# One more buffer for each gathered row: a ring of five places for U and ten for V, paid for by reloading shared rows

## The chip, the cores and the metric

One Trainium2 chip, one core. The metric is the device time of one execution in microseconds (us), lower is better. Each version is run several times, and medians are compared. The profile is one execution, recorded by the hardware profiler.

## The reference

Two transformer-like blocks work on 512 tokens of width 1024. Both end in the same kind of sparse mixer ("peer"), which is where nearly all bytes come from:

```
q = (xn @ w_q)                                    # 8 heads, two half keys each
s = q . sub_keys ; top 16 of each half, then top 16 of the 256 sums
es = expert numbers: 8 heads x 16 = 128 experts of each token, out of 16384
act = gelu(einsum('cd,ced->ce', xc, expert_u[ec]))       # 128 dot products of length 1024
out = einsum('ce,ced->cd', gate * act, expert_v[ec])      # weighted sum of 128 rows
```

Block 1 is `h + mixers(rms_norm(h))`, then `h + peer(rms_norm(h) * ln2_g)`, with an S5 state-space mixer and sliding-window attention (128 tokens back). Block 2 has compressed, selected and window attention and a short convolution; its outputs are scaled by rows that are computed from a condition vector (`gt1`, `sc2`, `sh2`, `gt2`): `x = x + gt1 * (mixed @ w_out)`, `h2 = rmsnorm(x, ln_ffn_g) * (1 + sc2) + sh2`, `x = x + gt2 * peer(h2)`, and the result is `rmsnorm(x, ln_final_g)`.

## The kernel before

**Tiles and slots.** The tokens are cut into tiles of 128, so there are eight tiles of work: n = 0 to 3 in layer 1, n = 4 to 7 in layer 2. Each tile needs 128 experts per token. One *slot* is one expert for all 128 tokens of a tile, 1024 slots in all. For slot s GpSimd (`gpsimd_program`) issues one indirect DMA that gathers 128 rows of 8 KB (the U row and the V row of an expert stand next to each other in HBM), 1.05 MB, into the ring. VectorE (`dot`) multiplies the U row with the tile's normed input and sums; ScalarE (`weigh`, for two slots at a time) applies GELU and the gate and makes a small diagonal matrix; TensorE (`vmm`) multiplies it with the V row and adds up in PSUM.

**The ring.** `ring` has NU + NV rows of 1024 numbers in each partition, with NU = 4 and NV = 2 NU. Slot s has its U row at `u_at(s)` and its V row at `v_at(s)`, one in front of the other or behind it in turn, so that one transfer fills both. The gather of slot s may be issued when dot(s - NU) and vmm(s - NV) are done.

**Order.** All five engines run through programs written out in advance. While the slots of tile n - 1 run, the dense work of tile n (norm, projections, attention, routing, top 16) is done in between: `place(n, part, f)` gives the slot at which each piece stands, from the tables `L1_PARTS` and `L2_PARTS`, and `pace` makes an engine do all slots up to there first. Each engine works strictly in its order, so a piece of dense work that takes long, or waits, holds up the slots behind it.

**Weights.** SyncE (`sync_program`) loads the dense weights as units of 512 KB into six places of `wsl`; unit k waits until unit k - 6 is used. `extra(k)` puts other loads in front of unit k, in the same queue.

**Rows.** Several rows of 1024 numbers are held broadcast over all partitions, 4 KB per partition each: `rowA` (the norm's gains, loaded once per layer and in layer 2 multiplied with 1 + sc2), `finr` (first scratch of the condition vector's work, then sc2 as `rsc2`, then the gains of the last norm), `gt1`, `rowB`, `gt2`. `route` makes the normed input X of the peer mixer from `hres` and `rowA`; `wout2` multiplies with `gt1`; `finish` and `finish2` make a finished tile of the output in `fin`, and scale it with `finr`. `kT1` holds the keys of all four tiles of layer 1; `pers` is a large buffer for what must stay.

Of the kernel before, what the change touches and what calls it, by code (L numbers as in the profile page):

```python
# [9 lines left out]
F32 = mybir.dt.float32  # L10
# [6 lines left out]
NU = 4  # L17
NV = 2 * NU
NWS = 6
NSLOT = 1024  # L20
PAIR = 2
# [78 lines left out]
def build(nc, A, out, act_counts):  # L100
    ctx = ExitStack()
    with ctx:
# [51 lines left out]
        finr = sb("finr", [128, D])  # L154
# [5 lines left out]
        rowA = sb("rowA", [128, D])  # L160
        rowB = sb("rowB", [128, D])
        big = sb("big", [128, 5120])
        pers = sb("pers", [128, 13312])
# [5 lines left out]
        modd = nc.dram_tensor("modd", [12, 512], F32, kind="Internal").ap()  # L169
        modr = modd.rearrange("(a b) c -> a (b c)", b=2)  # L170
# [12 lines left out]
        kT1, o = carve(pers, o, 2, 512)  # L183
# [6 lines left out]
        assert o <= 13312, o  # L190
# [38 lines left out]
        gt1, o = carve(pers, o, 1024)  # L229
# [18 lines left out]
        tmp2, o = carve(big, o, 512)  # L248
        gg = cols2[:, 0:24]
# [7 lines left out]
        rsc2 = finr[:, :]  # L257
        bmod = finr[:, 256:768].rearrange("p (b c) -> p b c", c=128)

        def route_bufs(blk):  # L260
            if blk:
                sS, o = carve(pers, at_route, 16, 128)
                halves, base = [sS[:, 0:8, :], sS[:, 8:16, :]], pers
            else:
                halves = [x[:, :].rearrange("p (a b) -> p a b", b=128) for x in (fin, gt2)]
                base, o = rowB, 0
            r = {"halves": halves}
            r["s2"], p = carve(base, o, 256)
            r["cand"], p = carve(base, p, 16, 16)
            r["oh"], o = carve(base, o, 2, 16, 16)  # L270
# [4 lines left out]
            assert o <= (13312 if blk else D), o  # L275
            return r
# [19 lines left out]
        mrow = [finr[:, 0:128], finr[:, 128:256]]  # L296
# [65 lines left out]
        def vector_program(v):  # L362
# [28 lines left out]
            def finish2(n):  # L391
                V.stage("fin")
                V.wait_ge("fsq", n)
                V(v.tensor_scalar(st[:, 2:3], st[:, 2:3], 1.0 / D, 1e-6, ALU.mult, ALU.add))
                V.wait_own()
                V(v.reciprocal(st[:, 2:3], st[:, 2:3]), ("frc", n))
                V.wait_ge("frs", n)
                V.wait_ge("finr")
                V(v.scalar_tensor_tensor(fin[:, :], fin[:, :], st[:, 2:3], finr[:, :], ALU.mult, ALU.mult),
                  ("fout", n))  # L400

            def slots(x):
                back = V.here
                while V.slot < x and V.slot < END:
# [7 lines left out]
                    if k == VL + 4 and n >= 5:  # L412
                        finish2(n - 1)
# [157 lines left out]
            def qk1(n):  # L571
# [26 lines left out]
                V(ts(kT1[:, :, 128 * i:128 * i + 128], PS[2][:, 0:256].rearrange("p (a b) -> p a b", a=2), kgc,  # L598
# [182 lines left out]
            def route(n):  # L781
# [10 lines left out]
                if n == 0:  # L792
                    V.wait_ge("rowA", 0)
                V(v.scalar_tensor_tensor(X, hres[:, i, :], st[:, 1:2], rowA[:, :], ALU.mult, ALU.mult),
# [252 lines left out]
            def wout2(n):  # L1047
# [19 lines left out]
                for b in range(2):  # L1067
# [5 lines left out]
                    V.wait_ge("modrow", 2)  # L1073
# [49 lines left out]
        def scalar_program(a):  # L1123
# [58 lines left out]
            def slots(x):  # L1182
                back = S.here
                while S.slot < x and S.slot < END:
# [9 lines left out]
                    if k == VL + 4 and n >= 5:  # L1194
                        finish2(n - 1)
# [118 lines left out]
            def route(n):  # L1314
# [5 lines left out]
                rstd(n, "r", 1, hres[:, i, :], xr[:, :])  # L1320
                pace(n, "route", 0.3)
# [134 lines left out]
        def tensor_program(t):  # L1456
# [143 lines left out]
            def scores1(n, g):  # L1600
# [8 lines left out]
                for r in range(4):  # L1609
                    k0 = 128 * (n - 1) + s0  # L1610
                    x = t.matmul(PS[r // 2][:, 256 * (r % 2) + s0:256 * (r % 2) + 256],
                                 xT[64 * a_:64 * a_ + 64, 4 * m + r, :],
                                 kT1[64 * a_:64 * a_ + 64, m, k0:128 * (n + 1)], start=True, stop=True)
# [335 lines left out]
        def sync_program(s):  # L1949
# [20 lines left out]
            def extra(k):  # L1970
# [7 lines left out]
                if (n, name, b, u) == (0, "glu", 0, 0):  # L1978
                    load(rowA[:, :], A["ln2_g"].broadcast_to([128, D]), "rowA", 0)
# [16 lines left out]
                if (n, name, b, u) == (4, "win", 3, 0):  # L1996
                    for q in range(4, 12):
                        Y.wait_ge("modo", q)
                    load(rsc2, modr[4:5, :].broadcast_to([128, 1024]), "modrow", 4)
                    Y.wait_ge("X", 3)  # L2000
                    load(rowA[:, :], A["ln_ffn_g_2"].broadcast_to([128, D]), "lnf")
# [7 lines left out]
                if n >= 4 and (name, b, u) == ("win", 4, 0):  # L2009
                    Y.wait_ge("h", n - 1, 1)  # L2010
                    Q(s.dma_start(cw, A["conv_w_2"][0, :, 0, :].unsqueeze(0).broadcast_to([128, 3, 512])), "cw",
                      ("cw", n))
                if (n, name, b, u) == (4, "wout", 0, 0):
# [4 lines left out]
                    load(gt1, modr[2:3, :].broadcast_to([128, 1024]), "modrow", 2)  # L2018
# [3 lines left out]
                if (n, name, b, u) == (5, "win", 0, 0):  # L2022
                    Y.wait_ge("rowA", 1)
                    load(finr[:, :], A["ln_final_g_2"].unsqueeze(0).broadcast_to([128, D]), "finr")
# [14 lines left out]
            for k in range(NWS, len(units)):  # L2039
                extra(k)  # L2040
                unit(k)

# [127 lines left out]
```

## Time and profile before

| what | before |
|---|---|
| median of 3 runs | 3549.24 us (3537.84 to 3552.84) |
| the profiled execution's own time | 3552.45 us |
| its span | 3551.0 us |
| moved by DMA | 1343.61 MB, 378 GB/s over the span |
| busy share TensorE / VectorE / ScalarE / GpSimd | 70 / 67 / 39 / 30% |

The page cuts the span into 40 slices and gives for each the share of time in which the core's 16 DMA engines were busy, and the GB/s that they moved. Tables by windows give the same for any stretch. Their DMA share is the sum of the packets' times over 16 engines; a few percent of overlap make it read up to 1.02 where no engine is idle. GpSimd is listed as POOL, VectorE as DVE, ScalarE as ACT, TensorE as PE (its weight loads as PEld), SyncE as SP.

### The profile page before, as it was taken

The page shows a single profiled execution, that of the slowest core. Times are in us where ns is not written, and L with a number is a line of the kernel's source. Part 1 is how long each engine was busy: PE and PEld are TensorE (multiplying, and loading weights), DVE is VectorE, ACT ScalarE, POOL GpSimd, SP SyncE. Part 2 cuts the span into 40 slices and gives each one's busy share as a digit, 9 for nine tenths or more (in the row PEclk, how much of TensorE's full clock was granted, in tenths as well). Part 3 has the DMA queues.
Part 4 walks back from the last instruction along what each step waited for, and adds up shares of the span by engine and source line. Part 5 has one row for each costly group of instructions (what it writes and reads, how often), then busy time and mean ns, then how long its engine had stood idle before and what let it go on. Part 6 is the DMA issues. An engine that isn't in the chain of part 4 may idle for free.

```text
span 3551.0 us, 40113 instructions
## 1 busy us (share of the span) xinstructions
PE 2498.8 (70%) x13640; PEld 977.6 (28%) x13640; DVE 2390.7 (67%) x5690; ACT 1370.3 (39%) x3648; POOL 1078.5 (30%) x1038
## 2 busy tenths in 40 slices
PE   7768669676696776866577667767677668765555
PEld 3433233222332223322222223222232223311111
DVE  7438873687835878467664886668775887666664
ACT  1113332344323443233283335534383436533332
POOL 0001332223322233332333323332333323333332
PEclk9689779798797987988778888888888888977777
DMA  7659999999999999999999999999999999999998
GB/s 241 218 200 375 369 355 406 416 408 393 359 396 416 416 391 355 385 394 396 380 409 395 399 398 394 395 400 414 374 401 393 393 394 401 387 386 393 396 407 336
DMA packets 228013, 1343.61 MB, mean 378 GB/s; under 512 B 28360, under 2 KB 33768, under 8 KB 95968
## 3 DMA queue, kind: packets, MB, share of 16 engines
q0 software_dynamic: 148320, 1076.50, 76.0%
q1 hardware_dynamic: 78816, 262.43, 19.3%
q8 instruction: 107, 1.75, 0.2%
q10 hardware_dynamic: 672, 2.12, 0.1%
q14 instruction: 98, 0.80, 0.1%
HBM read 1338.24 MB, written 2.71 MB: 378 GB/s over the span
## 4 chain that ended last, share of the span: by engine, by line
DMA 31%; PE 26%; DVE 17%; issue 15%; POOL 5%; ACT 4%; SPq 0%; POOLq 0%; ACTq 0%; DVEq 0%
DMA ring<-in_k_uv,idx 15%; PE ps L1543 12%; DMA ring<-in_k_vu,idx 12%; PE ps L1472 9%; DVE ring L372 6%; POOL ring L1944 5%; DMA wsl<-in_k_wu 4%; DVE big L420 2%; ACT L1128 1%; PE ps L1525 1%; PE ps L1681 1%; DVE rowB L420 1%; ACT diag L1128 1%; ACT xr L1128 1%; PE ps L1627 1%
## 5 line engine op out<-in xcount | busy, mean ns | idle before, releaser
L372 DVE CUSTOM_DVE_ANT_0 ring<-ring,xn 128x1024 f32<-128x1024 f32 x1024 | 1243.7, 1222 | 654.3 <-DMA ring<-in_k_uv,idx 351.7
L1472 PE MATMUL ps<-ring,diag 64*64 64x512 f32 x8192 | 1272.2, 741 | 518.9 <-ACT diag L1128 474.9
L1944 POOL DMA_INDIRECT ring<-in_k_vu,idx x512 | 530.7, 1036 | 1267.2 <-DVE aw L372 673.7
L1944 POOL DMA_INDIRECT ring<-in_k_uv,idx x512 | 541.7, 1058 | 1109.5 <-DVE aw L372 855.9
L1543 PE MATMUL ps<-wsl,xT 128*128 128x512 f32 (+1 forms) x1536 | 730.1, 622 | 77.9 <-DMA wsl<-in_k_wu 54.1
L1472 PEld LDWEIGHTS ps<-ring,diag 64*64 64x64 f32 x8192 | 304.8, 158 | 1240.8 <-ACT diag L1128 725.2
L1128 ACT ACTIVATE aw<-aw 128x2 f32<-128x2 f32 x512 | 103.9, 203 | 1320.1 <-DVE aw L372 1314.6
L1128 ACT ACT_TABLE_LOAD x375 | 481.1, 1283 | 64.2 <-DVE big L420 51.8
L1543 PEld LDWEIGHTS ps<-wsl,xT 128*128 128x128 f32 x1536 | 291.7, 200 | 528.1 <-issue 437.8
L1128 ACT ACTIVATE diag<-gid,aw 128x64 f32<-128x64 f32 x1024 | 306.3, 341 | 129.6 <-PE ps L1472 112.9
L1128 ACT ACTIVATE gid<-ident,gate 128x64 f32<-128x64 f32 x1024 | 292.5, 332 | 0.0
L1681 PE MATMUL ps<-pers,rowB 128*128 128x64 f32 x224 | 51.3, 421 | 106.1 <-DVE rowB L678 81.6
L1525 PE MATMUL ps<-ident,big 128*128 128x128 f32 x288 | 60.1, 332 | 81.9 <-DVE big L420 31.7
L420 DVE TENSOR_TENSOR big<-ps,big 128x512 f32<-128x512 f32 x40 | 27.6, 690 | 107.6 <-PE ps L1543 107.3
L1525 PE MATMUL ps<-ident,xr 128*128 128x128 f32 x208 | 37.1, 334 | 85.7 <-DVE xr L424 64.4
L372 DVE DVE_READ_ACCUMULATOR2_ANT aw<- 128x1 f32 x1024 | 83.9, 82 | 0.0
L1681 PEld LDWEIGHTS ps<-pers,rowB 128*128 128x128 f32 x224 | 48.7, 329 | 118.4 <-issue 118.4
L1525 PEld LDWEIGHTS ps<-ident,big 128*128 128x128 f32 x288 | 38.0, 164 | 137.3 <-ACT big L1128 60.6
L1128 ACT ACTIVATE xr<-ps 128x512 f32<-128x512 f32 x32 | 18.2, 589 | 144.6 <-PE ps L1543 141.1
L420 DVE TENSOR_TENSOR big<-big 128x512 f32<-128x512 f32 x84 | 58.2, 693 | 20.0 <-ACT big L1128 17.1
L1863 PE MATMUL ps<-pers,big 128*128 128x64 f32 x320 | 48.9, 288 | 23.9 <-DVE big L1024 23.9
L420 DVE TENSOR_TENSOR big<-ps,pers 128x512 f32<-128x512 f32 (+5 forms) x120 | 58.1, 494 | 3.5 <-PE ps L1627 2.8
(227 smaller groups left out, 2033.9 us busy)
## 6 DMA issues: line engine op xcount, KB each, us to landing
wsl<-in_k_wu SPq DMA_DIRECT2D x408, 512.0 KB
wsl<-in_k_wmod SPq DMA_DIRECT2D x48, 512.0 KB
ring<-in_k_vu,idx POOLq DMA_INDIRECT x512
ring<-in_k_uv,idx POOLq DMA_INDIRECT x512
wsl<-in_k_wu SPq DMA_DIRECT2D x16, 280.0 KB
big<-in_b_gate SPq DMA_DIRECT2D x4, 1024.0 KB, 11.7
big<-in_conv_w SPq DMA_DIRECT2D x4, 768.0 KB
hres<-in_x SPq DMA_DIRECT2D x4, 512.0 KB, 7.7
```

Of the source, the lines that this page charges most:

```text
L372: V(v.tensor_tensor_reduce(u_row(s), u_row(s), xn[:, b, :], 1.0, 0.0, ALU.mult, ALU.add, aw[:, b, k:k + 1]), ("dot", s))
L420: return v.tensor_tensor(out, a_, b_, op)
L1128: return a.activation(out, in_, f, **kw)
L1472: r = t.matmul(PA[half][64 * q:64 * q + 64, :], diag[64 * half:64 * half + 64, s % (2 * PAIR), :], v_row(s)[64 * half:64 * half + 64, 512 ...
L1525: r = t.transpose(PS[bank][:, j * 128:(j + 1) * 128], s_, ident[:, :])
L1543: r = t.matmul(PS[bank][:, 0:nn], lhsT(kk_), wsl[:, at % NWS, j, 0:nn], start=(kk_ == 0), stop=(kk_ == nk - 1))
L1627: x = t.matmul(PS[2 + b][:, 256 * h + 128 * z:256 * h + 128 * z + 128], BT[32 * j:32 * j + 32, 4 * z + c, :], uT[32 * j:32 * j + 32, c, :] ...
L1681: x = t.matmul(PS[4 + h // 8][:, 64 * (h % 8):64 * (h % 8) + 64], PT1[:, r, 128 * k:128 * k + 128], v1[:, (n + 1 + k) % 2, 64 * g:64 * g + ...
L1863: r = t.matmul(PS[4 + br][:, 64 * h:64 * h + 64], PT2[:, k % 2, 128 * j:128 * j + 128], vsn[:, j, 128 * br + 64 * g:128 * br + 64 * g + 64 ...
L1944: Q(p.indirect_dma_start(out=both_rows(s), out_offset=None, in_=tab, in_offset=bass.IndirectOffsetOnAxis(ap=idx[:, n % 2, k:k + 1], axis=0 ...
```

## The change

It raises NU from 4 to 5, so the ring has 15 rows for 12 (12 KB more in each partition). The room comes from four places:

- `rowA` is gone. The norm's gains are loaded anew for each tile into `fin` (called `lnr`), just before the unit `wq` 0 0. In layer 2 the product of gains and 1 + sc2 is made once, at tile 4; ScalarE writes it to DRAM (`lnd`), and tiles 5 to 7 load it from there.
- `finr` is gone. The gains of the last norm are loaded for tile 4 and tile 5 into `xr`, and once for tiles 6 and 7 into a place of `wsl` when the weights are used up. For tiles 4 to 6 `finish2` moves from slot 8 to slot 20 of the next tile.
- `gt1` no longer stays in `pers`; it is loaded for each tile of layer 2 into a part of `big` that attention uses, after attention is done (`o1`, n, 1). sc2 goes beside it at tile 4.
- `kT1` keeps two tiles of keys. In an odd tile they stand in order; in an even tile the two halves are swapped, and one score product of 256 columns becomes two of 128.

```diff
-NU = 4
+NU = 5
 NV = 2 * NU
...
-        kT1, o = carve(pers, o, 2, 512)
+        kT1, o = carve(pers, o, 2, 256)
...
+        gt1, _ = carve(big, o2 + 1024, 1024)
+        lnr = fin[:, :]
+        def finr(n):
+            return xr[:, :] if n < 6 else wsl[:, 0, :, :].rearrange("p a b -> p (a b)")
...
-                    if k == VL + 4 and n >= 5:
+                    if k == (20 if n < 8 else VL + 4) and n >= 5:
                         finish2(n - 1)
...
+                V.wait_ge("lnr", n)
                 if n == 4:
-                    V.wait_ge("lnf")
                     V.wait_ge("modrow", 4)
-                    V(v.scalar_tensor_tensor(rowA[:, :], rsc2, 1.0, rowA[:, :], ALU.add, ALU.mult), ("rowA", 1))
+                    V(v.scalar_tensor_tensor(lnr, rsc2, 1.0, lnr, ALU.add, ALU.mult), ("lnf",))
...
+                if n == 4:
+                    S.wait_ge("lnf")
+                    Q(a.dma_start(lnd, lnr[0:1, :]), "lnd", ("lnd",))
...
+                    if n % 2:
+                        x = t.matmul(PS[r // 2][:, 256 * (r % 2):256 * (r % 2) + 256], q,
+                                     kT1[64 * a_:64 * a_ + 64, m, :], start=True, stop=True)
+                    else:
+                        for k in range(s0 // 128, 2):
+                            x = t.matmul(PS[r // 2][:, 256 * (r % 2) + 128 * k:256 * (r % 2) + 128 * k + 128], q,
+                                         kT1[64 * a_:64 * a_ + 64, m, 128 * (1 - k):256 - 128 * k],
+                                         start=True, stop=True)
...
-                    load(gt1, modr[2:3, :].broadcast_to([128, 1024]), "modrow", 2)
...
+                if n >= 4 and (name, b, u) == ("wout", 1, 0):
+                    Y.wait_ge("o1", n, 1)
+                    Q(s.dma_start(gt1, modr[2:3, :].broadcast_to([128, 1024])), "gt1", ("gt1", n))
+                    if n == 4:
+                        load(rsc2, modr[4:5, :].broadcast_to([128, 1024]), "modrow", 4)
+                if (name, b, u) == ("wq", 0, 0):
+                    if n < 4:
+                        Y.wait_ge("s5b", n, 1)
+                        row = A["ln2_g"]
...
+                    else:
+                        Y.wait_ge("lnd")
+                        if n >= 6:
+                            Y.wait_ge("out", n - 2)
+                        row = lnd
+                    Q(s.dma_start(lnr, row.broadcast_to([128, D])), "lnr", ("lnr", n))
+                if n >= 6 and (name, b, u) == ("win", 4, 0):
+                    last_row(n - 2)
```

On SyncE's queue, from the second half of tile 5's input projection to that of tile 6's, before (`wsl` is the weights, `in_conv_w` the convolution's taps; the 33 units are 8 of win, 8 of wout, 8 of wq, 1 of sk, and 8 of the next tile's win):

```order
L2011 DMA big<-in_conv_w 128x1536
L1962 DMA wsl<-in_k_wu 128x1024 x33
L1962 DMA wsl<-in_k_wu 128x2x280 x4
L1962 DMA wsl<-in_k_wu 128x1024 x4
L2011 DMA big<-in_conv_w 128x1536
```

The same stretch of the changed kernel's SyncE queue, where `big<-modd` is gt1, `fin<-lnd` the norm's row and `xr<-in_ln_final_g` the last norm's gains for tile 4:

```order
L2021 DMA big<-in_conv_w 128x1536
L1974 DMA wsl<-in_k_wu 128x1024 x12
L2033 DMA big<-modd 128x1024
L1974 DMA wsl<-in_k_wu 128x1024 x4
L2048 DMA fin<-lnd 128x1024
L1974 DMA wsl<-in_k_wu 128x1024 x17
L1974 DMA wsl<-in_k_wu 128x2x280 x4
L1974 DMA wsl<-in_k_wu 128x1024 x4
L2021 DMA big<-in_conv_w 128x1536
L2055 DMA xr<-in_ln_final_g 128x1024
```

The run of 33 units is now cut in three: the second half of `wout` stands behind gt1 and its wait for the end of attention, and `wq` stands behind the norm's row.

In layer 1, the same queue from tile 0's GLU weights to the end of tile 1's units, before (`in_b_gate` is the gate's bias, `in_k_bmod` the condition vector's, `in_k_wmod` its weights):

```order
L1962 DMA wsl<-in_k_wu 128x1024 x41
L1989 DMA big<-in_b_gate 128x2048
L1962 DMA wsl<-in_k_wu 128x1024 x24
L1954 DMA finr<-in_k_bmod 128x512
L1962 DMA wsl<-in_k_wu 128x1024 x33
L1962 DMA wsl<-in_k_wmod 128x1024 x16
```

And in the changed kernel:

```order
L1974 DMA wsl<-in_k_wu 128x1024 x24
L2048 DMA fin<-in_ln_g 128x1024
L1974 DMA wsl<-in_k_wu 128x1024 x17
L2000 DMA big<-in_b_gate 128x2048
L1974 DMA wsl<-in_k_wu 128x1024 x24
L1966 DMA pers<-in_k_bmod 128x512
L1974 DMA wsl<-in_k_wu 128x1024 x24
L2048 DMA fin<-in_ln_g 128x1024
L1974 DMA wsl<-in_k_wu 128x1024 x9
L1974 DMA wsl<-in_k_wmod 128x1024 x16
```

One load of 512 KB has come in ahead of the nine units `wq` and `sk` of every tile.

## Rows read from the trace of the kernel before

**Rows 1.** The page: engines' busy time; DMA by slices; the gathers' queue.

```profile
PE 2498.8 (70%) x13640; PEld 977.6 (28%) x13640; DVE 2390.7 (67%) x5690; ACT 1370.3 (39%) x3648; POOL 1078.5 (30%) x1038
DMA  7659999999999999999999999999999999999998
GB/s 241 218 200 375 369 355 406 416 408 393 359 396 416 416 391 355 385 394 396 380 409 395 399 398 394 395 400 414 374 401 393 393 394 401 387 386 393 396 407 336
q0 software_dynamic: 148320, 1076.50, 76.0%
```

**Rows 2.** Windows: width, busy us by engine, PEclk, DMA share, GB/s.

```profile
267.00:3531.00 3264.00, 2302.64 (x12774) 875.05 (x12776) 2247.12 (x5324) 1320.62 (x3544) 1068.36 (x1020) 0.83 0.98 393
3233.00:3245.00 12.00, 7.06 (x36) 1.61 (x32) 5.17 (x11) 1.78 (x8) 3.75 (x5) 0.64 1.01 422
```

**Rows 3.** Windows around gaps of the DMA engines, three of 26.

```profile
402.00:408.00 6.00, 6.00 (x36) 1.99 (x29) 4.89 (x10) 2.09 (x8) 2.90 (x3) 0.69 0.53 172
...
1379.00:1386.00 7.00, 7.00 (x44) 3.47 (x44) 6.11 (x12) 2.44 (x10) 2.73 (x3) 0.79 0.52 186
...
3224.00:3229.00 5.00, 3.61 (x16) 0.80 (x16) 3.50 (x8) 3.10 (x8) 2.62 (x2) 0.54 0.63 218
```

**Rows 4.** Timeline, tile 1's attention, around 396 to 409 us.

```profile
396.77 0.94 POOL L1944 DMA_INDIRECT ring<-in_k_uv,idx  x1 [1.54 <-DVE aw L372]
...
397.96 3.65 PE L1681 MATMUL ps<-pers,rowB 128*128 128x64 f32 x16 [7.04 <-issue]
...
400.25 1.23 DVE L372 CUSTOM_DVE_ANT_0 ring<-ring,xn 128x1024 f32<-128x1024 f32 x1
...
401.54 5.73 PE L1472 MATMUL ps<-ring,diag 64*64 64x512 f32 x32
...
402.79 1.23 DVE L372 CUSTOM_DVE_ANT_0 ring<-ring,xn 128x1024 f32<-128x1024 f32 x1
...
404.33 1.24 POOL L1944 DMA_INDIRECT ring<-in_k_uv,idx  x1 [6.62 <-DVE aw L372]
```

**Rows 5.** Timeline, tile 6's convolution, around 2500 to 2512 us.

```profile
2500.63 1.22 DVE L372 CUSTOM_DVE_ANT_0 ring<-ring,xn 128x1024 f32<-128x1024 f32 x1
...
2502.12 1.15 POOL L1944 DMA_INDIRECT ring<-in_k_vu,idx  x1 [3.76 <-DVE aw L372]
...
2506.41 1.22 DVE L372 CUSTOM_DVE_ANT_0 ring<-ring,xn 128x1024 f32<-128x1024 f32 x1
...
2507.90 1.68 POOL L1944 DMA_INDIRECT ring<-in_k_vu,idx  x1 [4.63 <-DVE aw L372]
```

**Rows 6.** Waits of VectorE in tile 2's attention, 801 to 979 us: total, times, longest.

```profile
DVE ring L372 <- DMA ring<-in_k_vu,idx: 11.9, 11, 3.3
DVE ring L372 <- DMA ring<-in_k_uv,idx: 11.5, 15, 3.0
```

**Rows 7.** Timeline of GpSimd before and after the first dot product.

```profile
251.50 0.94 POOL L1944 DMA_INDIRECT ring<-in_k_vu,idx  x1 [0.30 <-issue]
286.67 0.94 POOL L1944 DMA_INDIRECT ring<-in_k_uv,idx  x1 [34.24 <-DVE aw L372]
```

**Rows 8.** Timeline, output projection and routing of tile 6.

```profile
2664.28 0.69 DVE L420 TENSOR_TENSOR big<-big 128x512 f32<-128x512 f32 x1
...
2675.87 15.99 SPq L1962 DMA_DIRECT2D wsl<-in_k_wu  x8
...
2683.16 3.70 PE L1543 MATMUL ps<-wsl,xT 128*128 128x512 f32 x8
...
2695.69 1.28 DVE L794 SCALAR_TENSOR_TENSOR xn<-hres,st,rowA 128x1024 f32<-128x1024 f32 x1 [1.16 <-ACT st L1128]
```

**Rows 9.** Issue to landing of the gate's bias; queues in 2680 to 2698 us.

```profile
big<-in_b_gate SPq DMA_DIRECT2D x4, 1024.0 KB, 11.7
...
q0 software_dynamic: 666, 4.86, 65.3%
q1 hardware_dynamic: 708, 2.60, 35.8%
```

More of the change, by code:

```diff
@@ L20 @@
 NSLOT = 1024
+PERS = 12192
 PAIR = 2
@@ L153, in build @@
         gt2 = sb("gt2", [128, D])
-        finr = sb("finr", [128, D])
         xT = sb("xT", [128, 8, 128])
@@ L159, in build @@
         cols3 = sb("cols3", [128, 2, 8])
-        rowA = sb("rowA", [128, D])
         rowB = sb("rowB", [128, D])
         big = sb("big", [128, 5120])
-        pers = sb("pers", [128, 13312])
+        pers = sb("pers", [128, PERS])
         rflat = ring[:, :, :].rearrange("p a b -> p (a b)")
@@ L189, in build @@
         snk, o = carve(pers, o, 16)
-        assert o <= 13312, o
+        mrow = [carve(pers, o + 128 * k, 128)[0] for k in range(2)]
+        bmod, o = carve(pers, o + 256, 4, 128)
+        assert o <= PERS, o
         gt, o = carve(big, 0, 2048)
@@ L228, in build @@
         zprev, o = carve(pers, o, 512)
-        gt1, o = carve(pers, o, 1024)
         at_route = o
@@ L255, in build @@
         o3 = o1r.rearrange("p (h d) -> p h d", d=64)
-        rsc2 = finr[:, :]
-        bmod = finr[:, 256:768].rearrange("p (b c) -> p b c", c=128)
+        rsc2, _ = carve(big, o2, 1024)
         def route_bufs(blk):
@@ L295, in build @@
         assert o <= 3328
-        mrow = [finr[:, 0:128], finr[:, 128:256]]
         first = [carve(rflat, 512 * k, 4, 128)[0] for k in range(3)]
@@ L397, in finish2 @@
                 V.wait_ge("frs", n)
-                V.wait_ge("finr")
-                V(v.scalar_tensor_tensor(fin[:, :], fin[:, :], st[:, 2:3], finr[:, :], ALU.mult, ALU.mult),
+                V.wait_ge("finr", n)
+                V(v.scalar_tensor_tensor(fin[:, :], fin[:, :], st[:, 2:3], finr(n), ALU.mult, ALU.mult),
                   ("fout", n))
@@ L1072, in wout2 @@
                     V.wait_ge("wout", n, b)
-                    V.wait_ge("modrow", 2)
+                    V.wait_ge("gt1", n)
                     V(tt(x, PS[4 + b], gt1[:, 512 * b:512 * b + 512], ALU.mult), ("wo_e", n, b))
@@ L1193, in slots @@
                         finish(n - 1)
-                    if k == VL + 4 and n >= 5:
+                    if k == (20 if n < 8 else VL + 4) and n >= 5:
                         finish2(n - 1)
@@ L1609, in scores1 @@
                 for r in range(4):
[L1610 to L1613, printed above, removed]
+                    q = xT[64 * a_:64 * a_ + 64, 4 * m + r, :]
+                    if n % 2:
[6 more added lines that the diff above has]
+                                         start=True, stop=True)
                 T(x, ("a_sc", n, g))
@@ L2010, in extra @@
                     Y.wait_ge("h", n - 1, 1)
+                    if n == 5:
+                        Y.wait_ge("lnf")
                     Q(s.dma_start(cw, A["conv_w_2"][0, :, 0, :].unsqueeze(0).broadcast_to([128, 3, 512])), "cw",
@@ L2021, in extra, with last_row @@
                     load(gt2[:, :], modr[5:6, :].broadcast_to([128, 1024]), "modrow", 5)
-                if (n, name, b, u) == (5, "win", 0, 0):
-                    Y.wait_ge("rowA", 1)
-                    load(finr[:, :], A["ln_final_g_2"].unsqueeze(0).broadcast_to([128, D]), "finr")
+                if n >= 4 and (name, b, u) == ("wout", 1, 0):
[7 more added lines that the diff above has]
+                        row = A["ln2_g"]
+                    elif n == 4:
+                        Y.wait_ge("gate", 3, 7)
+                        row = A["ln_ffn_g_2"]
+                    else:
[6 more added lines that the diff above has]
+                    last_row(n - 2)
+            def last_row(*tiles):
+                if tiles[0] < 6:
+                    Y.wait_ge("perm", tiles[0])
+                Q(s.dma_start(finr(tiles[0]), A["ln_final_g_2"].unsqueeze(0).broadcast_to([128, D])), "finr",
+                  *[("finr", n) for n in tiles])
             load(hres[:, 0, :], A["x"][0, 0:128, :], "x", 0)
@@ L2041, in sync_program @@
                 unit(k)
+            for k in range(len(units) - NWS, len(units)):
+                Y.wait_ge("unit_used", k)
+            last_row(6, 7)
         for engines in ((Blank(),) * 5, (nc.vector, nc.scalar, nc.tensor, nc.gpsimd, nc.sync)):
```

13 lines of the change are left out of this document (4 added, 9 removed).

## The prediction, made before the changed kernel ran

> **What bounds the kernel now.** I read the page first, for the busy shares. No compute engine is near full: VectorE is busy 67% of the span [rows 1]. The DMA row is another matter: nearly all slices after the third read 9, and the gathers (q0) alone take 76.0% of the 16 engines' span [rows 1]. So the next view is the windows. Between the first dot product and the last gather, 267 to 3531 us, the DMA share is 0.98 and the rate 393 GB/s; in a stretch without a gap the share reads 1.01 and the rate 422 GB/s [rows 2]. The kernel is bound by its bytes, 1077 MB of them gathered. What is left over is (a) a hundredth or two of the time in which DMA engines have nothing queued and (b) stretches at full share whose packets are slower than the best. A ring of more places can only win back (a).
>
> I then went through the span in narrow windows and looked for gaps. There are 26 of them between 400 and 3230 us: 12 in the attention of tiles 1 to 3 (four per tile, one for each group of heads), the others in layer 2's convolution, compression and output stages and in the last tile's top 16; [rows 3] show the first, the deepest and the last. A window loses its width times (1 - share): 6 x 0.47 = 2.8 us, 7 x 0.48 = 3.4 and 5 x 0.37 = 1.9 us. Summed in the same way the 26 give 58.7 us. The stretch as a whole loses 3264 x 0.02 = 65 us (share rounded to 0.01, so 49 to 82), so the gaps are nearly all there is of (a).
>
> The timeline tells why a gap opens. In tile 1's attention GpSimd issues a gather at 396.77 and the next at 404.33 us [rows 4], 7.6 us later, where one gather takes 1.05 MB / 422 GB/s = 2.5 us. The row names a dot product as releaser, but dots kept coming, at 400.25 and 402.79 for instance; what had been missing is on TensorE, where the attention's products stand at 397.96 and the late `vmm`s of four slots (8 matmuls each) follow in one block at 401.54 [rows 4]. The gather of s waits for vmm(s - 8). In tile 6's convolution it is VectorE: one dot at 2500.63, the next at 2506.41, the convolution's element-wise work in between, and GpSimd's issues lie 5.8 us apart [rows 5]. Both are bursts, no lack of capacity: in the 178 us of tile 2's attention with its four gaps VectorE still waits 11.9 + 11.5 = 23.4 us for gathered rows [rows 6]. It has time to catch up once the rows are there.
>
> **The change part by part.**
>
> *The ring.* With five U rows and ten V rows the gather of s waits for dot(s - 5) and vmm(s - 10). At the start of each burst one more gather is in flight, worth 2.5 us of DMA time, and two more slots of `vmm` may be late. A gap of g us becomes max(0, g - 2.5). Of the 26, twelve are longer than 2.5 us, by 4.0 us together (0.9 for the longest). So 58.7 - 4.0 = 54.7 us are won if each burst finds the ring full; the waits of [rows 6], 6 us for each gap, say that it does. At the other end, if TensorE's block of late `vmm`s only moves, half of that, 27 us. I take 54.7. Once, at the start, four gathers are issued by 251.50 and the fifth waits 34.24 us for the first dot [rows 7]; that one now comes early too: 2.5 us.
>
> *More bytes.* Before there are five broadcast loads of 512 KB among the rows concerned (rowA twice, gt1, sc2, finr). Now there are sixteen: 8 for the norm's row, 4 of gt1, 1 of sc2, 3 of the last norm's. Eleven more, all in the DMA-bound stretch: 11 x 0.524 MB / 393 GB/s = 14.7 us. These are paid in full, since nothing hides a byte where the DMA engines bound the time.
>
> *SyncE's waits.* The unit `wout` 1 0 and all behind it now stand behind o1(n, 1). In tile 6 attention ends at 2664.28 + 0.69 = 2664.97, and TensorE wants the second half of wout from 2683.16 on [rows 8]: 18.2 us. In this time gt1 and two units must land, 3 x 0.524 = 1.57 MB. Where both queues have work, SyncE's moves 2.60 MB in 18 us, 144 GB/s [rows 9], so 10.9 us. To this I add 4.4 us until its first bytes, an estimate from the gate's bias: 1.05 MB landed 11.7 us after its issue [rows 9], of which 1.05 / 0.144 = 7.3 us are the transfer. That leaves 2.9 us to spare. The next units were issued from 2675.87 on anyway [rows 8]. The norm's row comes after the unit issued second there: by its end 3.15 MB have gone since 2665, 21.9 + 4.4 us, at 2691.3; X is made at 2695.69 [rows 8], 4.4 us later. Cost taken as 0, cover thin. At tile 4 sc2 comes in addition, 3.6 us more, 0.7 us too late. The other waits (`s5b`, `out`, `gate` 3 7, `perm`) are for events that lie before the unit use that SyncE waits for in any case, so 0. In layer 1 the row goes behind the last unit of wout, whose use stands ahead of X by a matmul group and the residual sum: 0 beyond its bytes.
>
> *TensorE, ScalarE, VectorE.* Tile 2's scores cost 16 matmuls of 256 columns as 32 of 128, so 16 more instructions. The nearest row is a group of 8 matmuls of 512 columns in 3.70 us [rows 8], 0.46 us each, so between 0 and 16 x 0.46 = 7.4 us; four times wider products are far above it, and the ring now gives TensorE two slots more of cover: 0. `finish2` moves 12 slots on, with the same instructions: its result is waited for by the output transfer alone. One DMA issue on ScalarE: 0.
>
> The sum is made against the profiled execution's 3552.45 us, which lies 3.2 us above the median: 3552.45 - 54.7 - 2.5 + 14.7 = 3510.
>
> *A rule against it.* The gapless rate that I count on is 422 GB/s, and the mean 393 [rows 2]. The Trainium skill, page "DMA: Bandwidth & Descriptors", section "Bandwidth", gives 435 GB/s as the limit of SBUF's ports and about 358 GB/s as the core's share of HBM, and says that for transfers between HBM and SBUF the HBM side binds. By that rule the kernel would be past its limit and filling a gap would win nothing. The trace does not agree, since it holds 422.
>
> **The rivals.**
>
> A, as above: gaps filled, 3510 us. For it: bursts, idle time of VectorE on DMA, 26 gaps of about one gather's length.
>
> B, half of it: in the attention TensorE's block is late by more than two slots, or filling a gap lets the next burst find the ring no fuller, so that half the gain comes: 3552.45 - 27 - 2.5 + 14.7 = 3537. For it: [rows 4] has four `vmm`s in a block, and the extra place covers two. Against: GpSimd needs only one issue more per gap.
>
> C, the memory side is the limit on the average: gaps vanish from the share, but packets get slower with one more gather queued, and the bytes need the same time plus the new ones: 3552.45 + 14.7 = 3567, a loss of 0.4 to 0.5%. For it: slices that read 9 and move 385 to 396 GB/s [rows 1]. Against: 422 at 1.01 [rows 2]. The rule cited above would lead here.
>
> D, the thin cover fails, the case of the other side: with five gathers queued SyncE's queue gets less than its 144 GB/s. At half of that, the 3.15 MB up to the norm's row need 44 + 4.4 us, X of each tile of layer 2 comes at 2713.4 instead of 2695.69, and VectorE holds all dots behind it: 17.7 us for each of 4 tiles, 3510 + 71 = 3581. It decides (slower than 3567) from 14 us per tile on. Against: when dots stop, gathers stop, and SyncE's queue then has all 16 engines, so the delay limits itself.
>
> **How the numbers follow.** A measurement of this kernel can tell about 0.5% (18 us) from no change; the bounds are 3531 and 3567. Chances: A 0.66, B 0.14, C 0.10, D 0.10. A's own range is 3490 to 3530: below, the shallow losses outside the 26 gaps (65 - 59 us, up to 82 by rounding) come back too; above, 2 or 3 of 10 gaps stay open. B gives 3530 to 3550, mostly within 0.5%. C ends at the edge of "same" and "slower". Faster 0.70 (A, a little of B), same 0.18, slower 0.12. The range that leaves out no more than 2 in 10 reaches from 3484 to 3550: A, B and the unknown above and below.
>
> **What the profile after would show.** The windows at the same stages (about 1% earlier as the span goes on) should read 0.9 and more where [rows 3] read 0.5 to 0.6, and the share from first to last slot 0.99 or 1.00. GpSimd's issues in the attention should lie 7 us apart still, but with the DMA share high between them. The rate without gaps should stay near 420 GB/s; if it falls while the share rises, C. VectorE's waits for the ring should shrink in the attention and not elsewhere. In layer 2, the wait of VectorE for the norm's row before X, and of TensorE for `wsl` at the second half of wout, should be under 2 us; 10 us or more there is D. The bytes should come to 1343.6 + 5.8 = 1349.4 MB. The forecast is wrong if gaps of 2 us remain in the attention, or if the added loads land late.

## The result, and the profile after

The changed kernel takes 3432.36 us (median of 4, 3428.02 to 3438.13), the kernel before 3551.04 us in the same rounds (median of 4, 3537.84 to 3561.72). The ratio is 0.9669, its interval 0.9632 to 0.9705: 118 us less by the ratio, where 42 were forecast (3552.45 to 3510), and below the forecast range of 3484 to 3550. The profiled execution took 3428.02 us.

The page of the changed kernel: span, busy time, DMA in 40 slices, and the two large queues (q0 the gathers, q1 SyncE's loads: packets, MB, share of 16 engines' span). It answers to [rows 1].

```profile
span 3426.5 us, 40200 instructions
...
PE 2462.4 (72%) x13672; PEld 962.9 (28%) x13672; DVE 2380.6 (69%) x5690; ACT 1368.1 (40%) x3646; POOL 1122.9 (33%) x1038
...
DMA  7669999999999999999999999999999999999997
GB/s 247 210 219 367 405 411 410 416 393 411 409 404 416 416 411 407 410 417 404 396 419 413 414 392 409 418 417 413 399 419 416 413 402 419 417 418 409 420 418 328
...
q0 software_dynamic: 148320, 1076.50, 77.0%
q1 hardware_dynamic: 80400, 268.20, 20.4%
```

The windows of the changed kernel, with the columns of [rows 2]: first dot product to last gather, a stretch without a gap, tile 1's attention, tile 6's convolution, and three gaps that are left, in the convolutions of tiles 5, 6 and 7.

```profile
267.00:3406.00 3139.00, 2268.17 (x12794) 863.08 (x12792) 2234.81 (x5319) 1317.90 (x3541) 1111.83 (x1019) 0.85 1.01 410
3200.00:3212.00 12.00, 7.42 (x48) 1.68 (x40) 8.25 (x22) 2.88 (x12) 4.45 (x5) 0.78 1.01 421
...
391.00:397.00 6.00, 5.46 (x28) 4.16 (x32) 5.93 (x10) 0.55 (x2) 1.56 (x2) 0.50 1.01 416
397.00:403.00 6.00, 6.00 (x60) 2.78 (x56) 4.50 (x10) 2.09 (x8) 4.05 (x3) 0.94 1.01 421
2416.00:2422.00 6.00, 4.18 (x20) 2.17 (x24) 5.76 (x10) 1.27 (x5) 1.15 (x1) 0.50 1.00 393
...
2037.00:2042.00 5.00, 4.11 (x29) 0.99 (x32) 4.97 (x11) 2.44 (x11) 3.66 (x2) 0.75 0.42 126
2422.00:2427.00 5.00, 4.46 (x24) 0.96 (x21) 4.96 (x13) 2.75 (x12) 3.71 (x3) 0.50 0.51 169
2802.00:2808.00 6.00, 3.79 (x28) 2.05 (x28) 5.86 (x10) 1.44 (x7) 2.08 (x2) 0.83 0.62 233
```

The slices say it at once: the digits of the DMA row are the same 9s as in [rows 1], yet the GB/s under them stand at 404 to 420 nearly everywhere, where [rows 1] have many of 355 to 395. The gap of [rows 3] in tile 1's attention (share 0.53) now reads 1.01, and the stretch from first dot to last gather moves 410 GB/s for 393. The rate without a gap is as before, 421 for 422 [rows 2].

Not every gap is closed. The twelve of the attention are (no window of 5 us there reads below 0.89), but in the convolutions of tiles 5, 6 and 7 the last three windows above still read 0.42, 0.51 and 0.62, a loss of 2.9, 2.5 and 2.3 us. Before, the same three stages lost 2.8, 2.7 and 2.9 us (shares 0.54, 0.55 and 0.51 over 6 us each). In tile 6 the dots before the gap start at 2408.87, 2415.40 and 2421.19 us, two pauses of VectorE in a row; why one place more changes so little there was not tested.

The timeline of GpSimd in the burst of tile 1's attention, which answers to [rows 4]:

```profile
392.85 1.27 POOL L1956 DMA_INDIRECT ring<-in_k_uv,idx  x1 [1.56 <-DVE aw L378]
...
397.91 1.15 POOL L1956 DMA_INDIRECT ring<-in_k_uv,idx  x1 [3.79 <-DVE aw L378]
...
399.36 1.97 POOL L1956 DMA_INDIRECT ring<-in_k_vu,idx  x1 [0.30 <-PE ps L1479]
```

GpSimd still idles 3.79 us in the burst, its issues lie 5.1 us apart, and the one after comes right behind a `vmm` on TensorE (L1479): the waits are still there, but with five gathers ahead of them the DMA engines don't run dry.

**Where the 124.5 us between the two profiled spans lie.** A queue's share times the span is the time of 16 engines that its packets took; what is left of the span is idle (the shares are printed to 0.1%, so each figure is good to some 2 us, the last row to some 4). Packets overlap a little, since a stretch without a gap reads 1.01, so the idle time proper is some 1% of the span more in both columns.

| us | before | after | difference |
|---|---|---|---|
| gathers, the same 1076.50 MB | 76.0% x 3551.0 = 2698.8 | 77.0% x 3426.5 = 2638.4 | -60.4 |
| SyncE's loads, 262.43 MB, then 268.20 | 685.3 | 699.0 | +13.7 |
| other queues | 14.2 | 17.1 | +2.9 |
| nothing on the engines | 152.7 | 72.0 | -80.7 |

Of the 141 us won, 81 are idle time, as forecast in kind. The other 60 are that the same gathers took less engine time, 2.45 us per MB for 2.51; no term of the forecast stood for that. The added loads take 14 back. The other queues moved the same bytes but for 0.01 MB, so their 3 us are rounding.

### The profile page after: what moved, and what is told of

Same layout as the page of the kernel before. It is cut to its first block, busy times and chain, and to the rows that moved or that the text cites. A ratio compares the mean times of both kernels' runs of the same rounds, so it can differ in the third digit from the quotient of the medians.

```text
span 3426.5 us, 40200 instructions
## 1 busy us (share of the span) xinstructions
PE 2462.4 (72%) x13672; PEld 962.9 (28%) x13672; DVE 2380.6 (69%) x5690; ACT 1368.1 (40%) x3646; POOL 1122.9 (33%) x1038
## 2 busy tenths in 40 slices
DMA packets 229599, 1349.38 MB, mean 394 GB/s; under 512 B 28537, under 2 KB 33945, under 8 KB 97554
## 3 DMA queue, kind: packets, MB, share of 16 engines
q0 software_dynamic: 148320, 1076.50, 77.0%
q1 hardware_dynamic: 80400, 268.20, 20.4%
## 4 chain that ended last, share of the span: by engine, by line
DMA 31%; PE 25%; DVE 18%; issue 15%; POOL 6%; ACT 4%; POOLq 0%; ACTq 0%; DVEq 0%
DMA ring<-in_k_uv,idx 13%; PE ps L1550 12%; DMA ring<-in_k_vu,idx 10%; PE ps L1479 8%; DMA wsl<-in_k_wu 8%; DVE ring L378 7%; POOL ring L1956 6%; DVE big L426 2%; ACT L1132 1%; PE ps L1532 1%; PE ps L1693 1%; DVE rowB L426 1%; PE ps L1639 1%; ACT diag L1132 1%; ACT xr L1132 1%
## 5 line engine op out<-in xcount | busy, mean ns | idle before, releaser
L1479 PE MATMUL ps<-ring,diag 64*64 64x512 f32 x8192 | 1243.1, 727 | 422.1 <-ACT diag L1132 384.4
L1956 POOL DMA_INDIRECT ring<-in_k_vu,idx x514 | 558.7, 1087 | 1157.5 <-DVE aw L378 805.3
L1956 POOL DMA_INDIRECT ring<-in_k_uv,idx x510 | 558.1, 1094 | 1048.1 <-DVE aw L378 789.0
L1550 PE MATMUL ps<-wsl,xT 128*128 128x512 f32 (+1 forms) x1536 | 734.5, 623 | 106.3 <-DMA wsl<-in_k_wu 84.7
L1479 PEld LDWEIGHTS ps<-ring,diag 64*64 64x64 f32 x8192 | 301.1, 155 | 1129.4 <-ACT diag L1132 627.1
L1550 PEld LDWEIGHTS ps<-wsl,xT 128*128 128x128 f32 x1536 | 290.8, 200 | 557.8 <-issue 414.4
L426 DVE TENSOR_TENSOR big<-big 128x512 f32<-128x512 f32 x84 | 58.1, 692 | 20.0 <-ACT big L1132 17.1
L1715 PE MATMUL ps<-wsl,cact 128*32 128x128 f32 x768 | 36.3, 326 | 45.5 <-DMA wsl<-in_k_wmod 32.3
## 6 DMA issues: line engine op xcount, KB each, us to landing
wsl<-in_k_wmod SPq DMA_DIRECT2D x48, 512.0 KB, 17.1
```

The costliest lines, as they stand in the source:

```text
L426: return v.tensor_tensor(out, a_, b_, op)
L1479: r = t.matmul(PA[half][64 * q:64 * q + 64, :], diag[64 * half:64 * half + 64, s % (2 * PAIR), :], v_row(s)[64 * half:64 * half + 64, 512 ...
L1550: r = t.matmul(PS[bank][:, 0:nn], lhsT(kk_), wsl[:, at % NWS, j, 0:nn], start=(kk_ == 0), stop=(kk_ == nk - 1))
L1715: r = t.matmul(mod_bank(b)[32 * j:32 * j + 32, 0:128], cact[:, 2 * k0 + k, :], wsl[:, at % NWS, k, 128 * j:128 * j + 128], start=(k0 + k = ...
L1956: Q(p.indirect_dma_start(out=both_rows(s), out_offset=None, in_=tab, in_offset=bass.IndirectOffsetOnAxis(ap=idx[:, n % 2, k:k + 1], axis=0 ...
```

## The experiments

Every run but `g1_gathers_alone` and `f2_finish2_alone` is an edit of the changed kernel. The runs were made on several chips, so I compare ratios to the kernel before (one hundredth is 35.5 us); the changed kernel's is 0.9669.

**1. The changed kernel with the old waits.** All else stays: layout, loads, keys.

```diff
-if s >= NU:     G.wait_ge("dot", s - NU)
-if s >= NV:     G.wait_ge("vmm", s - NV)
+if s >= NU - 1: G.wait_ge("dot", s - NU + 1)
+if s >= NV - 2: G.wait_ge("vmm", s - NV + 2)
```

> The changed kernel with its 15-row ring, all its added loads and its five semaphores, but the gather of slot s waits for dot(s-4) and vmm(s-8) as before. Theory 1 (lead): a gather that is issued late, with little queued ahead of it, has slower packets, so depth alone gives both the closed gaps and the faster full-share stretches; then all is lost again and the added bytes are paid: 3551 + 14 = 3565 us, 3550 to 3575. Theory 2 (layout): the slow packets came from the old ring's addresses or the old placement of the rows; then only the gaps return: 3432 + 47 to 60, 3480 to 3495 us, and windows at full share keep 410 to 420 GB/s.

Measured 3560.21 us (10 runs), ratio 1.0004 (0.9993 to 1.0015). Page of this run, the two queues, and its window from the first dot to 3400 us (its last gather is issued at 3532 us):

```profile
q0 software_dynamic: 148320, 1076.50, 75.6%
q1 hardware_dynamic: 80400, 268.20, 19.7%
```

```profile
267.00:3400.00 3133.00, 2221.63 (x12363) 857.67 (x12362) 2169.63 (x5175) 1280.13 (x3399) 1008.46 (x967) 0.84 0.98 393
```

The whole gain is gone, the rate is back at 393 GB/s, and the gathers take 75.6% x 3559.1 = 2690.7 us again. What wins is how far GpSimd may run ahead, nothing in the layout by itself.

**2. A ring of four places in the changed kernel,** with its extra loads, keys and waits.

```diff
-NU = 5
+NU = 4
```

> The changed kernel with NU = 4: a 12-row ring, everything else of the change kept. It prices the eleven added loads, SyncE's new waits and the two-tile key buffer alone. The prediction's term: +14.7 us for bytes and 0 for waits, 3551 + 15 = 3566 us (3555 to 3580). Theory 1 expects it equal to the run with waits 4 and 8 on the 15-row ring within 8 us; theory 2 expects that one about 75 us faster than this.

3558.95 us, ratio 1.0006 (0.9991 to 1.0020), the same as run 1. The other parts of the change together cost 2 us (-3 to +7), not 14.7.

**3 and 4. One wait each.** The first keeps `vmm` at s - 10 and waits for dot(s - 4); the second keeps dot at s - 5 and waits for `vmm`(s - 8).

```diff
-if s >= NU:     G.wait_ge("dot", s - NU)
+if s >= NU - 1: G.wait_ge("dot", s - NU + 1)
```

> Only the wait on the dot product is tightened to dot(s-4); vmm(s-10) stays. If TensorE's late products were what opened the gaps in layer 1 and VectorE's bursts those in layer 2, this keeps the first and loses the second. Theory 1: between the two, about 3510 us (3480 to 3540), with more of the gain lost in layer 2. Theory 2: 3450 to 3475 us, since only some gaps return.

```diff
-if s >= NV:     G.wait_ge("vmm", s - NV)
+if s >= NV - 2: G.wait_ge("vmm", s - NV + 2)
```

> Only the wait on the weighted sum is tightened to vmm(s-8); dot(s-5) stays. Theory 1: between the two, about 3500 us (3470 to 3540), with more of the gain lost in layer 1's attention and in the output and routing stages, where TensorE is late. Theory 2: 3450 to 3475 us.

3516.33 us, ratio 0.9884 (0.9856 to 0.9913), and 3516.91 us, ratio 0.9880 (0.9862 to 0.9898). Either alone gives 41 to 43 us, both 118. My reading is that where both dots and `vmm`s are late, relaxing one wait shows nothing. Windows of tile 1 with its attention (356 to 534 us) and of much of layer 2, before (the later window holds slightly different work in each run, since the faster ones are further on):

```profile
356.00:534.00 178.00, 112.95 (x743) 54.68 (x744) 141.02 (x256) 69.88 (x209) 64.04 (x61) 0.76 0.93 361
1780.00:3115.00 1335.00, 974.71 (x5416) 379.69 (x5416) 936.69 (x2266) 649.45 (x1620) 458.70 (x437) 0.85 0.99 396
```

changed:

```profile
356.00:534.00 178.00, 135.47 (x826) 61.12 (x830) 142.83 (x261) 73.64 (x220) 77.54 (x65) 0.83 1.00 408
1780.00:3115.00 1335.00, 971.74 (x5515) 372.57 (x5515) 967.25 (x2347) 623.96 (x1614) 480.38 (x448) 0.86 1.01 412
```

more V rows only (`e2_u_waits_4`):

```profile
356.00:534.00 178.00, 127.67 (x798) 59.22 (x799) 143.90 (x261) 72.11 (x215) 70.08 (x64) 0.80 0.97 390
1780.00:3115.00 1335.00, 957.45 (x5409) 374.14 (x5408) 930.91 (x2263) 625.58 (x1587) 451.81 (x431) 0.86 0.99 398
```

more U rows only (`e3_v_waits_8`):

```profile
356.00:534.00 178.00, 115.38 (x770) 54.41 (x770) 141.85 (x258) 70.84 (x207) 65.41 (x60) 0.75 0.93 369
1780.00:3115.00 1335.00, 976.21 (x5534) 380.25 (x5526) 945.80 (x2293) 653.58 (x1643) 479.47 (x444) 0.87 1.00 406
```

In tile 1 the V rows bring 29 of the 47 GB/s and the U rows 8: TensorE's late `vmm`s hold the ring there. In layer 2 it is the other way, 2 and 10 of 16: VectorE's dots hold it. These are the two kinds of burst of [rows 4] and [rows 5].

**5. Gathers alone, a fixed number in flight.** The kernel leaves the whole reference out; its output is what the buffers hold. GpSimd gathers from the same table, 96 slots each with k = 1 to 6 in flight, then k = 3 to 6 with SyncE's loads beside them.

```diff
+for k, count in [(k, 96) for k in (1, 2, 3, 4, 5, 6)] + [(k, 96) for k in (3, 4, 5, 6)]:
+    for j in range(count):
+        p.wait_ge(land[(s - k) % 6], 16 * ((s - k) // 6 + 1))    # gather s - k has landed
+        p.indirect_dma_start(...)
```

> Nothing of the reference: only gathers of the same kind (128 rows of 8 KB each, indices at random) with a fixed number k in flight, 96 each of k = 1, 2, 3, 4, 5, 6, and then 96 each of k = 3, 4, 5, 6 with loads of 512 KB on SyncE's queue beside them; its output is what lies in the buffers. Lead theory: the rate rises with k well past the point at which the DMA share reads about 1, that is k = 2 reads a share near 1 at below 400 GB/s, and k = 3 and more 415 to 422 GB/s. If the slow packets have nothing to do with the lead, the rate at share 1 is the same for every k. With loads beside them, SyncE's queue should move about 144 GB/s at every k, if depth does not change the turns (the prediction's case D wants this to fall with k).

It took 3205.64 us (one execution). The loads end during the last part, so "beside loads" is measured for k = 3, 4 and 5. Its windows for k = 1, 2, 3, 4, 5 and 6 in turn (width, GpSimd busy, PEclk, DMA share, GB/s):

```profile
20.00:540.00 520.00, 86.71 (x93) 1.00 0.52 186
560.00:820.00 260.00, 85.23 (x91) 1.00 0.97 366
840.00:1065.00 225.00, 83.71 (x90) 1.00 1.01 417
1085.00:1310.00 225.00, 83.22 (x89) 1.00 1.01 422
1330.00:1550.00 220.00, 81.47 (x87) 1.00 1.01 422
1570.00:1790.00 220.00, 82.17 (x88) 1.00 1.01 422
```

The queues of the same run, in the windows of k = 2 and k = 5 alone, then of k = 3 and k = 5 with loads beside them, 340 us each:

```profile
q0 software_dynamic: 13069, 95.23, 97.3%
...
q0 software_dynamic: 12748, 92.85, 101.3%
...
q0 software_dynamic: 12985, 94.57, 66.8%
q1 hardware_dynamic: 13000, 47.34, 35.0%
...
q0 software_dynamic: 12997, 94.62, 67.0%
q1 hardware_dynamic: 12991, 47.31, 34.8%
```

The second window (k = 2) is the one to learn from. With two gathers in flight the DMA engines look busy, share 0.97, and move 366 GB/s: a MB takes 0.973 x 260 / 95.23 = 2.66 us of 16 engines, with five in flight 1.013 x 220 / 92.85 = 2.40 us. A queue that is short of gathers shows up as slow packets before it shows up as a gap. And beside loads of SyncE the gathers' number doesn't matter: SyncE gets 47.3 MB in 340 us, 139 GB/s, at k = 3 and at k = 5. The two queues move nearly the same number of packets there (12985 and 13000), and a gather's packets hold twice the bytes.

**6 and 7. 12.6 MB more,** 48 loads of 256 KB into a spare buffer from SyncE, on the ring of five and on the ring of four.

```diff
+if k % 8 == 0 and k > 80:
+    if m: Y.wait_ge("spare", m - 1)
+    Q(s.dma_start(spare[:, :], A["k_wu0"][...]), "spare", ("spare", m)); m += 1
```

> The changed kernel with 48 further loads of 256 KB (12.6 MB, never used) spread over SyncE's queue. The prediction's price of bytes (12.6 MB at 393 to 415 GB/s) is 30 to 32 us on 3432, up to 40 because rows of 2 KB are slower: 3462 to 3472. If added loads are absorbed by idle time, as the ring of four seems to have done with 5.8 MB, under 10 us.

> The ring of four (with the change's loads) and the same 48 further loads, 12.6 MB, never used. With five places they cost 29 us. If a shallow ring leaves idle engines that added bytes can use, they cost less here: 5 to 20 us on 3559, 3564 to 3579. If bytes cost the same at every depth, 3588; then the near-zero price of the change's own 5.8 MB needs another reason.

Ring of five: 3461.62 us, ratio 0.9715 (0.9693 to 0.9737), 0.0046 or 16 us over the changed kernel, with the ends of the two intervals 4 us below it and 37 above. Ring of four: 3591.64 us, ratio 1.0097 (1.0067 to 1.0126), 0.0091 or 32 us over run 2 (17 to 48 in the same way). At the forecast's price of 393 GB/s 12.6 MB are 32 us. In the queue sums of the profiled executions SyncE's loads cost 32 more on five (731.4 for 699.0 us) and 36 more on four (733.0 for 697.0), and idle time hardly moves (72.0 to 72.8; 149.3 to 154.5); on five the profiled executions are the slowest of the one kernel's four and the fastest of the other's, which exaggerates the difference in their spans. So idle time swallows no bytes at either depth, and that is no reason for run 2's low price.

**8 and 9. A place more, paid with places of `wsl`.** Three places of weights, with five and with six of U.

```diff
-NWS = 6
+NWS = 3
```

> The changed kernel with three places for weight units instead of six (12 KB free): the control for the next. TensorE will wait for weights more often. If the DMA engines bound the time it should cost little, 3440 to 3480 us.

```diff
-NU = 5
+NU = 6
-NWS = 6
+NWS = 3
```

> Three places for weights and a ring of six for U and twelve for V. Against the control with five: what is left of gaps and slow packets is some 20 + 30 us, so a further place should win half of that, 15 to 35 us, if depth still counts; 0 to 5 if five places are enough.

3641.02 us, ratio 1.0222 (1.0188 to 1.0255), and 3623.82 us, ratio 1.0175 (1.0148 to 1.0202). Halving `wsl` costs 196 us, where the expectation was 3440 to 3480 us; so the time is not set by the bytes alone, which are the same. The sixth place wins about 17 of the 196 (the intervals overlap slightly, though in the same rounds all four times of six places lie below all four of five). What `n5_w3`'s weights cost, waits over the whole run (total, times, longest):

```profile
PE ps L1550 <- DMA wsl<-in_k_wu: 338.4, 150, 15.8
```

The same view of the changed kernel, with TensorE's wait for ScalarE's diagonals and GpSimd's for the `vmm`s, which runs 12 to 14 need:

```profile
PE ps L1479 <- ACT diag L1132: 384.4, 187, 8.3
...
POOL ring L1956 <- PE ps L1479: 262.8, 139, 12.4
...
PE ps L1550 <- DMA wsl<-in_k_wu: 85.0, 42, 15.5
```

**10 and 11. Room from elsewhere.** Small buffers move into `xr` and `cact`; that pays for a seventh place of `wsl`, or for six places of U with four of `wsl`.

```diff
-NWS = 6
+NWS = 7                # run 11: NWS = 4, NU = 6
-PERS = 12192
+PERS = 12096
-        big = sb("big", [128, 5120])
+        big = sb("big", [128, 4864])
-        kcc, o = carve(pers, o, 32)
-        hv, o = carve(pers, o, 2, 32)
+        kcc, _ = carve(cflat, 0, 32)
+        hv, _ = carve(cflat, 32, 2, 32)
-        c1, o = carve(big, o, 512)
+        c1, _ = carve(xr, 0, 512)
-        tmp2, o = carve(big, o, 512)
+        tmp2, _ = carve(xr, 0, 512)
```

> The changed kernel with seven places for weight units; the room comes from two scratch rows that move into xr and two small buffers that move into cact. Three places cost 209 us against six, so TensorE's wait for weights, with the weighted sums queued behind it, matters. TensorE still waits 85 us for units in the changed kernel. Expected: 10 to 30 us less than the changed kernel, 3402 to 3422. If the DMA engines alone bound it, within 5 us of 3432.

> The same room spent on the ring: six places for U, twelve for V, but four for weights. The sixth place was worth 17 us at three weight places; going from six to four should cost some 60 to 100 us. Expected 3470 to 3520, slower than the changed kernel.

Five and seven: 3424.93 us (3422.37 to 3427.23), ratio 0.9629 (0.9601 to 0.9656). It is the fastest median, 7 us below the changed kernel (14 by the ratios), but the ratios' intervals overlap, so it is ahead in name only; 10 to 30 us were expected. Six and four: 3491.66 us, ratio 0.9816 (0.9785 to 0.9848), 52 us over the changed kernel. With full weight places a sixth place of U would show whether five is enough; there was no room, and it wasn't tried.

**12 to 14. How late the weighted sum stands.** `vmm` of slot s stands VL slots behind its dot: three, five, and five with seven places of `wsl`.

```diff
-VL = 4
+VL = 3                 # run 13: VL = 5; run 14: VL = 5 and the edit of run 10
```

> The changed kernel with VL = 3: TensorE's weighted sum of a slot stands one slot earlier in its program, so V rows come free one slot sooner, as if the V ring were one longer, but TensorE gets to it before ScalarE is done more often and then waits with dense work behind. If the V ring is what still ends late, 5 to 20 us faster (3412 to 3427); if the waits of TensorE for ScalarE win, 10 us or more slower.

> The changed kernel with VL = 5: the weighted sum of a slot stands one slot later on TensorE, so V rows come free a slot later, and TensorE waits less for ScalarE. If TensorE's waits weigh more (VL = 3 lost 75 us), 5 to 30 us faster than 3432; if the V ring's lead does, 20 to 50 us slower, towards the run with vmm(s-8), 3517.

> Seven weight places and VL = 5 together. If both help they add up: 3400 to 3415; if VL = 5 hurts alone, it hurts here by the same amount.

VL = 3: 3507.00 us, ratio 0.9864 (0.9837 to 0.9892), 69 us more. TensorE then waits longer for the diagonals, 539.4 for 384.4 us, and everything behind in its order waits with it. Waits of this run:

```profile
PE ps L1479 <- ACT diag L1132: 539.4, 227, 8.6
```

VL = 5: 3451.07 us, ratio 0.9693 (0.9667 to 0.9719), and with seven places 3438.57 us, ratio 0.9657 (0.9628 to 0.9686). Neither is below its partner with VL = 4, and neither interval is clear of it. I had hoped for a gain from 5; there is none. The wait moves instead of going away. With VL = 5 TensorE waits 105 us less for the diagonals, but GpSimd waits 211 us more for the `vmm`s and only 185 us less for the dots (1594.3 to 1409.1 us):

```profile
POOL ring L1956 <- PE ps L1479: 474.1, 188, 15.6
...
PE ps L1479 <- ACT diag L1132: 279.1, 128, 7.9
```

**15. finish2 alone.** The kernel before, with `finish2` of tiles 4 to 6 moved from slot 8 to slot 20.

```diff
-                    if k == VL + 4 and n >= 5:
+                    if k == (20 if n < 8 else VL + 4) and n >= 5:
```

> The kernel before with one edit: finish2 of tiles 4 to 6 at slot 20 of the next tile instead of slot 8. The prediction took 0 for it. If it is what pays for the added bytes in the ring of four, it is 8 to 12 us faster than before; if not, within 3 us, and the cheap bytes stay unexplained.

3556.51 us against 3561.19, ratio 0.9993 (0.9977 to 1.0009): 2.5 us less, which is no difference. It doesn't pay for the 12.7 us between the forecast price of the loads and that of run 2.

## Why the prediction was off

**Right: what bounds the kernel, and by which mechanism it moves.** The bytes set the time as long as the engines keep the queue fed (run 8 shows the limit of that), and bursts like those of [rows 4] and [rows 5] starve the ring. Rival B (half) and rival C (slower packets once gaps are filled) are out: packets got faster. The gapless rate is 421 GB/s, as before. The Trainium skill's rule ("DMA: Bandwidth & Descriptors", "Bandwidth") that about 358 GB/s of HBM bind, under which filling gaps wins nothing, is not borne out: the changed kernel holds 410 GB/s over 3139 us, and run 5 422. The same section of the Trainium skill gives the 358 as what each core gets when both cores of a pair stream, and 425 GB/s as measured with the other core idle; the forecast left that condition out. This kernel runs on one core, and its 422 agrees with the second figure.

**Wrong: "A ring of more places can only win back (a)".** This is the step that failed. It took stretches at full share with slow packets, (b), for a property of the memory, and gave them 0. The gathers' engine time fell by 60 us. Run 5 shows why the split was false: packets are slower when few gathers are in flight (2.66 us per MB at k = 2, 2.40 at k = 5) while the share still reads 0.97. Run 1 ties it to this kernel: with the old waits, and nothing else changed, the gathers' 2638 us become 2691 again, 52 of the 60. The evidence had stood in [rows 1], slices of 9 that move 385 to 396 GB/s; the forecast quoted them as support for rival C, and they were the same starvation, only milder. Windows of 5 us show it: the kernel before spends 610 us at shares of 0.90 to 0.99, where it moves 370 GB/s, the changed one 199 us; where the share reads 1.00 and more, the two are nearly alike, 413 and 415 GB/s. So hardly any packets were slow at a truly full share. A digit of 9 covers both, and 0.98 must be read against the 1.01 of a gapless stretch.

**Too small: the idle time won back.** "The stretch as a whole loses 3264 x 0.02 = 65 us" measured it against a share of 1.00. A stretch without a gap reads 1.01 [rows 2], so the loss was 3264 x (1.01 - 0.98) = 98 us (84 when summed over windows of 5 us, with less rounding), and the 26 gaps (58.7 us) were not nearly all of it. Idle time fell by 81 us, where 54.7 + 2.5 = 57 were forecast. This term was 24 us too small; the many shallow dips between the gaps are the rest. In the other direction, the rule that a gap of g us becomes max(0, g - 2.5) failed in the three convolutions shown above, where it would have left 0.2 to 0.4 us each.

**Too large by run 2, right by the queue: the bytes.** "Paid in full" is right for the queue: SyncE's loads took 13.7 us more, 14.7 forecast, and the bytes came out at 1349.38 MB, 1349.4 forecast. But on a ring of four the loads, waits and keys together cost 2 us (-3 to +7) in time, and in its profiled execution the loads took 11.7 us more with 3.4 less each of gathers and of idle time, which lie near the rounding of the shares. Why is open. It isn't `finish2` (run 15), nor does idle time take bytes in (runs 6 and 7).

With those sizes the sum over the profiled executions is -60 - 81 + 14 + 3 = -124 us.

**Right at 0: SyncE's waits.** In tile 6, rows of the changed kernel's timeline that answer to [rows 8] (end of attention, issue of gt1 and of the norm's row, second half of wout, X, and the first products of wq):

```profile
2568.09 0.69 DVE L426 TENSOR_TENSOR big<-big 128x512 f32<-128x512 f32 x1
2568.80 0.33 SPq L2033 DMA_DIRECT2D big<-modd  x1
...
2581.77 1.08 SPq L2048 DMA_DIRECT2D fin<-lnd  x1
...
2586.97 3.70 PE L1550 MATMUL ps<-wsl,xT 128*128 128x512 f32 x8
...
2599.50 1.28 DVE L798 SCALAR_TENSOR_TENSOR xn<-hres,st,fin 128x1024 f32<-128x1024 f32 x1 [1.16 <-ACT st L1132]
...
2624.85 1.98 PE L1550 MATMUL ps<-wsl,xT 128*128 128x512 f32 x4 [1.46 <-DMA wsl<-in_k_wu]
```

gt1 goes out 0.02 us after attention ends, TensorE starts the second half of wout 18.2 us later, as forecast, without a wait, and X waits only for ScalarE's statistics, not for the row; over all eight tiles VectorE waits before X seven times, 8.1 us together, each time for ScalarE. One wait of 1.46 us for weights stands at wq. Over the whole run TensorE's waits for `wsl` (L1550) grow from 54.1 to 85.0 us, but the added loads and waits don't do that: run 1 has 45.3 and run 2 44.6. They come with the longer lead of the gathers (run 4, where only the wait for the dots is relaxed, has 82.2); why is not shown. Rival D needed SyncE's queue to be squeezed by a fifth gather. It wasn't, neither here (2.51 MB in 18 us, 139 GB/s; 144 in [rows 9]) nor in run 5. The queues of the changed kernel in 2584 to 2602 us:

```profile
q0 software_dynamic: 681, 4.96, 66.8%
q1 hardware_dynamic: 683, 2.51, 34.5%
```

**Half right: the waits of VectorE.** In tile 2's attention they shrink from 11.9 and 11.5 us [rows 6] to these, beside its waits for TensorE, waits in 770 to 948 us:

```profile
DVE big L426 <- PE ps L1550: 10.8, 2, 5.8
DVE gt L426 <- PE ps L1623: 7.0, 3, 2.9
...
DVE ring L378 <- DMA ring<-in_k_vu,idx: 4.0, 5, 1.3
...
DVE ring L378 <- DMA ring<-in_k_uv,idx: 0.8, 2, 0.5
```

In this stretch TensorE's products, not the ring, are now what VectorE waits for most. The forecast had these waits unchanged elsewhere, and there they shrink too: outside the attention of tiles 1 to 3, from 576 to 486 us.

## What to carry to other kernels

A DMA share a few hundredths below that of the best stretch doesn't say that the DMA engines give all they can: set the microseconds of engine time per MB (share x width / MB) beside those of the best stretch of the same trace, and test whether more transfers in flight win the difference. When two waits guard one ring, relaxing one may win a third of what both win, so test them together as well as apart. Room for depth must not come from a buffer that another engine needs as deep: here three places of `wsl` cost 196 us and a place of the ring gave back 17.

## What the runs showed of the hardware

- Gathers of 1.05 MB (128 rows of 8 KB) move 186 GB/s with one in flight, 366 with two, 417 with three and 422 with four to six (run 5). One alone takes 1.05 MB / 186 GB/s = 5.6 us from one to the next, 3.1 us more than at the full rate; GpSimd's issue of it, 0.94 us, is within that.
- With gathers and loads of SyncE both queued, the packets go one to one and the bytes two to one with three, four and five gathers in flight: 94.6 MB and 47.3 MB in 340 us, 278 and 139 GB/s, 417 together (run 5).
- That packets are slower with two gathers in flight is measured; what inside a packet's time makes it so is not, and stays open.
